# Three 256-column products of a weight tile onto one accumulator instead of a 512- and a 256-column product onto two halves

## The reference

```
hn = rmsnorm(x)
z, xbc, dt, u, g_a, g_b = split(hn @ w_in)
y_a = mamba2(z, silu(causal_conv(xbc)), dt) ; y_b = s5(u)
h  = x + (sigmoid(g_a) * y_a + sigmoid(g_b) * y_b) @ w_out
h  = h + (silu(gate) * val) @ w_down,   gate, val = causal_conv(rmsnorm(h) @ w_up)
out = rmsnorm(h)
```

## Time and profile before

| | us |
|---|---|
| three runs | 1672.95, 1673.08, 1673.11 |
| profiled execution | 1673.03 |
| its span, first to last instruction | 1671.3 |
| PE busy | 1661.6 |
| DVE busy | 1315.7 |
| ACT busy | 984.2 |
| mean granted clock of TensorE | 0.999 of full |

### The profile page before, as it was taken

One profiled execution on the slowest core, in us unless ns is written; L12 is line 12 of the kernel. 1 busy time (PEld: TensorE's weight loads), 2 busy tenths in 40 slices (PEclk: granted clock), 3 DMA queues, 4 the chain that ended last, 5 costly groups with the idle time before them and its releaser, 6 DMA issues.

```text
span 1671.3 us, 24189 instructions
## 1 busy us (share of the span) xinstructions
PE 1661.6 (99%) x8216; PEld 1386.3 (83%) x8216; DVE 1315.7 (79%) x1723; ACT 984.2 (59%) x1365; POOL 234.9 (14%) x337
## 2 busy tenths in 40 slices
PE   9999999999999999999999999999999999999998
PEld 8888888888888888888888888888888888888886
DVE  7999999999999996545766868888878888845544
ACT  7676676666677877444547754444444454454554
POOL 7843342221111110000000200000000000000001
PEclk9999999999999999999999999999999999999999
DMA  7666766666857666666787577777777777766564
GB/s 255 214 196 197 207 202 202 191 196 180 248 201 252 218 223 205 197 192 208 243 254 223 176 233 241 237 245 243 243 244 242 243 233 243 232 190 198 191 189 127
DMA packets 182873, 361.61 MB, mean 216 GB/s; under 512 B 17520, under 2 KB 45456, under 8 KB 182672
## 3 DMA queue, kind: packets, MB, share of 16 engines
q1 hardware_dynamic: 169264, 340.23, 64.0%
q0 software_dynamic: 12336, 19.92, 5.1%
q10 hardware_dynamic: 1200, 0.53, 0.1%
HBM read 335.41 MB, written 18.92 MB: 212 GB/s over the span
## 4 chain that ended last, share of the span: by engine, by line
PE 74%; DVE 2%; ACT 1%; issue 0%; DVEq 0%
PE psum L1930 23%; PE psum L1931 23%; PE psum L1932 23%; PE psum L1915 2%; PE psum L1917 1%; PE psum L2051 1%; DVE wlo L1216 1%; PE psum L2052 0%; DVE dec L1566 0%; ACT whi L740 0%; PE psum L2058 0%; PE psum L1966 0%; DVE dec L1562 0%; ACT xtok L949 0%; DVE zx L1629 0%
## 5 line engine op out<-in xcount | busy, mean ns | idle before, releaser
L740 ACT ACTIVATE whi<-raw 128x1024 fp32r<-128x1024 f32 x580 | 612.6, 1058 | 583.2 <-PE psum L1932 472.0
L1216 DVE TENSOR_TENSOR wlo<-raw,whi 128x1024 fp32r<-128x1024 f32 x580 | 708.8, 1228 | 312.6 <-ACT whi L740 305.9
L1915 PE MATMUL psum<-act,whi 128*128 128x512 f32 x1088 | 342.5, 396 | 0.0
L1930 PE MATMUL psum<-whi,nw 128*128 128x512 f32 x704 | 274.1, 389 | 0.0
L1931 PE MATMUL psum<-wlo,nw 128*128 128x512 f32 x704 | 273.9, 389 | 0.0
L1932 PE MATMUL psum<-whi,nw 128*128 128x512 f32 x704 | 273.9, 389 | 0.0
L1917 PEld LDWEIGHTS psum<-act,wlo 128*128 128x128 f32 x1088 | 204.4, 188 | 48.3
L1917 PE MATMUL psum<-act,wlo 128*128 128x256 f32 x1088 | 213.7, 278 | 0.0
L1915 PEld LDWEIGHTS psum<-act,whi 128*128 128x128 f32 x1088 | 165.6, 189 | 3.3 <-issue 3.2
L1932 PEld LDWEIGHTS psum<-whi,nw 128*128 128x128 f32 x704 | 132.1, 188 | 27.6
L1930 PEld LDWEIGHTS psum<-whi,nw 128*128 128x128 f32 x704 | 132.1, 188 | 27.3
(11 more groups left out here) (255 smaller groups left out, 2236.7 us busy)
## 6 DMA issues: line engine op xcount, KB each, us to landing
raw<-in_w_up SPq DMA_DIRECT2D x176, 512.0 KB, 4.8
raw<-in_w_zx SPq DMA_DIRECT2D x96, 512.0 KB, 3.7
raw<-in_w_down SPq DMA_DIRECT2D x88, 512.0 KB, 4.3
raw<-in_w_gate SPq DMA_DIRECT2D x64, 512.0 KB, 5.2
raw<-in_w_proj SPq DMA_DIRECT2D x48, 512.0 KB, 4.4
raw<-in_w_bc SPq DMA_DIRECT2D x32, 512.0 KB, 3.9
raw<-in_w_glu SPq DMA_DIRECT2D x32, 512.0 KB, 4.5
raw<-in_w_out SPq DMA_DIRECT2D x32, 512.0 KB, 4.7
```

Of the source, the lines that this page charges most:

```text
L740: fn(whi[:, s, :], raw[:, s, :], ACTF.Copy).then_inc(hi_ready, 1)
L1216: V.tensor_tensor(wlo[:, s, :], raw[:, s, :], whi[:, s, :], ALU.subtract).then_inc(lo_ready, 1)
L1915: mm(psum[:, b + t, :], whi[:, s, cols(t)], x, start=first, stop=False)
L1930: mm(banks[:, t, :], x_hi, high[:, k], start=first and k == 0, stop=False)
```

## The change

In `unit`, the 512-column matmul of the `whi` tile becomes two matmuls of 256 columns, first x_hi, then x_lo, and all products of a tile go onto the same 256 columns of PSUM. So a step is six matmuls of 256 columns. ScalarE copies the finished sums from PSUM straight to their place (for z, it applies SiLU in that pass), and increments `sum_ready` itself. The 36 VectorE adds and the semaphores `hsum_ready` and `z_done` go. At the end of `out`, VectorE adds the sums to `h` in one operation and waits for TensorE's `unit_used` alone.

```diff
-            def take_hsum(g, end, gi=0, ui=0):
+            def take_sums(to, g, end, gi=0, ui=0, func=ACTF.Copy):
 
                 act.wait_ge(unit_used, ui + end)
-                if g:
-                    act.wait_ge(sum_ready, gi + g)
-                fn(hsum[:, :, :], sums(g, 1), ACTF.Copy).then_inc(hsum_ready, 1)
+                fn(to, sums(g), func).then_inc(sum_ready, 1)
...
+            def group_sums(name, i, r):
+
                 _, per, quads, u0, g0 = phase(name)
-                take_hsum(g0 + r, u0 + (r + 1) * quads, i * per, i * (per * quads))
+                func = ACTF.Copy
+                if name == "u":
+                    to = ub[:, 2 * (r + 1):2 * (r + 1) + 2, :]
+                elif name == "zx" and r % 2 == 0:
+                    to, func = zx[:, ds(i * 4 + r, 2), 0, :], ACTF.Silu
+                elif comes_late(name, i, r):
+                    to = bc[:, i * 4 + r, :, :]
+                else:
+                    to = cpad[:, :, 3:3 + L]
+                take_sums(to, g0 + r, u0 + (r + 1) * quads, i * per, i * (per * quads), func)
...
-                if name == "zx" and r % 2 == 0:
-                    act.wait_ge(sum_ready, i * per + (g0 + r + 1))
-                    to = zx[:, ds(i * 4 + r, 2), 0, :]
-                    fn(to, to, ACTF.Silu).then_inc(z_done, 1)
...
-            def add_halves(to, g, gi=0):
-
-                dve.wait_ge(hsum_ready, gi + (g + 1))
-                V.tensor_tensor(to, sums(g, 0), hsum[:, :, :], ALU.add).then_inc(sum_ready, 1)
...
-                dve.wait_ge(hsum_ready, g + 1)
-                mul(hg, hg, hsum[:, :, :], ALU.add)
-                V.tensor_tensor(hg, sums(g, 0), hg, ALU.add).then_inc(sum_ready, 1)
+                dve.wait_ge(unit_used, UNIT0[name] + 4 * r + 4)
+                V.tensor_tensor(hg, sums(g), hg, ALU.add).then_inc(sum_ready, 1)
...
+                    x_hi, x_lo = x[:, 0:L], x[:, L:2 * L]
                     for t in tiles:
-                        mm(psum[:, b + t, :], whi[:, s, cols(t)], x, start=first, stop=False)
+                        mm(psum[:, b + t, 0:L], whi[:, s, cols(t)], x_hi, start=first, stop=False)
+                        mm(psum[:, b + t, 0:L], whi[:, s, cols(t)], x_lo, start=False, stop=False)
                     for t in tiles:
-                        ins = mm(psum[:, b + t, L:2 * L], wlo[:, s, cols(t)], x[:, 0:L], start=False, stop=last)
+                        ins = mm(psum[:, b + t, 0:L], wlo[:, s, cols(t)], x_hi, start=False, stop=last)
```

More of the change, by code:

```diff
@@ L242, in build_program @@
         dec_in = [sem("dec_in0"), sem("dec_in1")]
-        hi_ready, lo_ready, unit_used, hsum_ready, sum_ready = map(
-            sem, ("hi_ready", "lo_ready", "unit_used", "hsum_ready", "sum_ready"))
+        hi_ready, lo_ready, unit_used, sum_ready = map(
+            sem, ("hi_ready", "lo_ready", "unit_used", "sum_ready"))
         dve_step, act_step, pool_step, const_ready = map(sem, ("dve_step", "act_step", "pool_step", "const_ready"))
@@ L268, in build_program @@
         tap_ready = sem("tap_ready")
-        z_done, conv_done, xbc_done, cb_ready, scan_ready, exp_ready, m_ready, y_ready = map(
-            sem, ("z_done", "conv_done", "xbc_done", "cb_ready", "scan_ready", "exp_ready",
+        conv_done, xbc_done, cb_ready, scan_ready, exp_ready, m_ready, y_ready = map(
+            sem, ("conv_done", "xbc_done", "cb_ready", "scan_ready", "exp_ready",
                   "m_ready", "y_ready"))
@@ L303, in group_bank, with sums @@
             return 2 * (g % 2)
-        def sums(g, half):
+        def sums(g):
             b = group_bank(g)
-            return psum[:, b:b + 2, half * L:half * L + L]
+            return psum[:, b:b + 2, 0:L]
         def chunk_banks(name, c):
@@ L781, in _ @@
                 split_hi(n)
-            take_hsum(0, 4)
-            def group_hsum(name, i, r):
+            take_sums(ub[:, 0:2, :], 0, 4)
+            def group_sums(name, i, r):
                 _, per, quads, u0, g0 = phase(name)
-                take_hsum(g0 + r, u0 + (r + 1) * quads, i * per, i * (per * quads))
+                func = ACTF.Copy
[8 more added lines that the diff above has]
+                take_sums(to, g0 + r, u0 + (r + 1) * quads, i * per, i * (per * quads), func)
             def normed_hi(c):
@@ L814, in _ @@
                     if r >= 2 and j == 0:
-                        group_hsum("u", 0, r - 2)
+                        group_sums("u", 0, r - 2)
                     if j == 1:
@@ L858, in group_silu @@
                 _, per, quads, u0, g0 = phase(name)
-                if name == "u":
+                if name == "u" or name == "zx" and r % 2 == 0:
                     return
-                if name == "zx" and r % 2 == 0:
-                    act.wait_ge(sum_ready, i * per + (g0 + r + 1))
-                    to = zx[:, ds(i * 4 + r, 2), 0, :]
-                    fn(to, to, ACTF.Silu).then_inc(z_done, 1)
-                elif name == "zx":
+                if name == "zx":
                     act.wait_ge(conv_done, i * 2 + (r // 2 + 1))
@@ L896, in mixer_turn @@
                     last = name == "bc" and i == 1 and r == per - 1
-                    group_hsum(*before)
+                    group_sums(*before)
                     hi(0)
@@ L955, in gate_turn @@
                 if prev is None:
-                    group_hsum("bc", 1, 3)
+                    group_sums("bc", 1, 3)
                     hi(0)
@@ L988, in gate_turn @@
                     act.wait_ge(xbc_done, 18)
-                    act.wait_ge(z_done, 12)
+                    act.wait_ge(sum_ready, GROUP0["bc"])
                 hi(5)
@@ L1104, in _ @@
                 out_tail(s)
-                if s in (27, 31):
-                    take_hsum(GROUP0["out"] + s // 4 - 6, UNIT0["out"] + s + 1)
             def take_blocks(c, cc):
@@ L1295, in u_group @@
                 return GROUP0["u"] + r - 1 if r else GROUP0["u0"]
-            def u_sums(r):
-                add_halves(ub[:, 2 * r:2 * r + 2, :], u_group(r))
             def u_scaled(r):
@@ L1306, in lo @@
                 split_lo(UNIT0["u"] + j)
-            u_sums(0)
             dve.wait_ge(dt_half, 2)
@@ L1328, in _ @@
             V.reciprocal(s5p[:, 15, :], s5p[:, 14, :]).then_inc(s5_inv, 1)
-            u_sums(1)
             lo(9)
@@ L1336, in _ @@
             lo(12)
-            u_sums(2)
             normed(3)
@@ L1422, in s5_out @@
                 V.scalar_tensor_tensor(to, to, col("s5_d", blk), sums_at, ALU.mult, ALU.add).then_inc(y5_out, 1)
[L1424 to L1433, removed]
             def group_conv(name, i, r):
@@ L1467, in late_add @@
                     ins.then_inc(conv_done, 1)
[L1469 to L1474, removed]
             def x_turned(g):
@@ L1500, in mixer_turn @@
                     lo(0)
-                    if r or start:
-                        group_sums(*before)
                     s5_turn_back(r, blk * 4 + (r + 1), blk, start and r == 0)
@@ L1516, in mixer_turn @@
                         lo(2)
-                    cpad_free(*before)
                     s5_turn_on(r)
@@ L1520, in mixer_turn @@
                         last_state_sum(blk)
-                    if r == per - 1 and not last:
-                        group_sums(name, i, r)
                     if not last:
@@ L1586, in gate_turn @@
                     lo(0)
-                    group_sums("bc", 1, 3)
                     s5_out(7, YS5_LAST)
@@ L1623, in gate_turn @@
                     dve.wait_ge(xbc_done, 18)
-                    dve.wait_ge(z_done, 12)
+                    dve.wait_ge(sum_ready, GROUP0["bc"])
                 dve.wait_ge(y_ready, i * 2 + 2)
```

## The result

The changed kernel takes 1686.13 us (median of 6 runs, 1685.75 to 1686.40), the kernel before took 1673.09 us beside it (6 runs, 1672.80 to 1673.17). The ratio is 1.0078, with a 95% interval of 1.0065 to 1.0091: slower by 13 us, where the prediction had 1669.5 and a range up to 1677. The profiled execution has a span of 1684.0 us, and a mean granted clock of 0.998 of full against 0.999. Another execution of the changed kernel had 0.999 and took 1686.07 us, so the clock took no part.

The account below looks back on a forecast made before the run. The prediction took TensorE's matmul stream to bound the kernel, with no other engine holding it up. Profiled 1673.03 us, - 3.1 for the stream, - 0.4 for a removed wait, gave 1669.5 us; range 1663.5 to 1677.

Parts of the forecast that it names:

- A step after the change: Prediction's step pricing all six 256-column matmuls like L1917's, 0.1152 us each: 0.6914 us a step instead of 0.6965.
- the term of -3.1 us: TensorE's matmul stream: 0.0051 us saved in each of 608 steps.
- the far end: Slow case of 0.120 us for each matmul of a step, 1687 us in all; chance 3%.
- the fast rival: New 256s stream at half of `glu`'s 512, 0.1134 us; step 0.680, gain 9.8 us, 1662.8 us; chance 12%.
- its upper end: Upper bound on the matmul price from L1917's longest pair, 0.24 us: step 0.720 us, +14 us.
- the formula of the Trainium skill: Matmul distance N/2.4 ns plus fixed 2.5 ns: step from 650 to 655 ns, 608 steps cost 3.0 us more.
- What bounds the kernel: Claim that TensorE bounds the kernel, with 74% of the chain, and no other engine holds it up.
- Each matmul has a price of its own: Slower rival in the steps: two 256s 0.0036 us dearer than one 512, +4.4 us, 1677.0 us; chance 13%.
- The instruction stream: Slower rival: larger loop bodies of `zx` and `bc` cost 7 us at five jumps back, 1676.5 us; chance 5%.
- The wait of L2010: TensorE's 0.4 us wait for the sum into `cpad`, to go because ScalarE's copy frees the banks earlier.
- The relief: Less helper work, some 25 us on VectorE and 8.5 us on ScalarE, forecast to have no effect on time.
- The helpers' term of 0.4 us: Gain of 0.4 us forecast from removing TensorE's wait at L2010 for the sum into `cpad`.

Follow-up runs that it names:

- e1: Kernel before with only the 512-column matmul cut into two of 256, accumulator halves and VectorE adds kept: 1686.13 us, ratio 1.008.
- e3: Kernel before plus, before the end of `out`, unused streams of 24 matmuls per width (512 to 128 columns) and mixed steps in two orders: 1723.18 us.
- e5: Changed kernel with a step's six matmuls reordered so no tile is loaded twice in a row and accumulators alternate: 1685.99 us, ratio 1.008 against the kernel before.
- e7: Kernel before with each 512-column matmul of `glu` and `proj` cut into two of 256, 960 more matmuls: 1686.22 us, ratio 1.008.
- e2: Changed kernel with the old 512-column matmuls; ScalarE copies, no VectorE adds, W_hi·x_lo left out of the sums: 1672.39 us, ratio 0.9996 against the kernel before.
- e10: Changed kernel with 64 instead of 128 loaded columns in 532 of 608 steps: 1665.07 us, ratio 0.995 against the kernel before.
- e8: Kernel before plus unused streams of 24 matmuls by width and load size, then eight times two 512s and eight 256s: 1730.18 us.
- e9: Kernel before with 64 instead of 128 loaded columns in 532 of 608 steps: 1674.22 us, ratio 1.0005.
- e4: Kernel before with a step's four matmuls ordered 512, 256, 512, 256 instead of 512, 512, 256, 256: 1678.2 us, ratio 1.003.

## Why the prediction was wrong

**The step that failed** is the one under "A step after the change": "so 0.1152 is already the price with nothing saved up, and I take it for all six". A stream of nothing but such matmuls runs at 120 ns (the changed kernel, e1, e3, e5, e7), so the term of -3.1 us was +13.5; this is the far end that the prediction had worked out as 1687 and gave 3%. The 0.1152 was a correct reading of two distances and a wrong price: the step of 696.5 ns was divided at the borders of the rows, which made the 512s 233.0 and the 256s 115.2. Streams of one kind give 226.9 and 119.9, and 3.1 for the mixture: 453.8 + 239.8 + 3.1 = 696.7. The change trades this for 6 x 120 = 720: four 256s for two 512s, +26, and the mixture's 3 back.

**The rows allowed the other division.** `glu` had the 512 in a pure stream, 0.2268. Taking it out of the step twice leaves (696.5 - 453.6) / 2 = 121.5 for a 256, and six of those make +20 us. The prediction used that row to argue for the fast rival, that the 512s could be freed of a slowness, and took the price from single distances where it should have kept both divisions of the sum. It had 0.24 / 2 as its upper end, which is what came, and set it aside. For the same reason it dismissed the formula of the Trainium skill against the split: it held two 256s of the mixed step, 0.2305 us, against one 512 of it, 0.2330. The pure streams say 239.8 ns against 226.9, so the formula had the sign right, and with 3.0 us a loss four times too small.

**What bounds the kernel** was read rightly, on thinner ground than the prediction says. The chain with 74% TensorE begins at 378 us and says nothing of `u`, `zx` and half of `bc`, where 1007 of the 1216 matmuls of L1915 stand; there the reading rests on the waits alone. The runs bear it out: e1 has the whole loss with the helpers as they were, and e2, with the new helpers and the old matmuls, has none.

**The rivals.** "Each matmul has a price of its own" was right in its kind, wrong in its size and in its supposed reason: no reload of x_lo's tile is involved (e5), and nothing of the activation's side (e7). The fast rival is refuted for whole tiles: what the 512s gain by leaving the mixture is 3.1 ns a step. That half tiles give its 113 and its 0.680 (e10) goes with the smaller load. The instruction stream did not run dry: 3.8 us of "issue" in 10 waits against 4.6 in 9, and no gap at the jump.

**What held.** Loads and matmuls, 9432 each. The wait of L2010, gone, though not for the reason given: it is gone in e1 too, where the helpers are as before. No effect of the helpers (e2). Untouched token-major stages: 226.7 ns from start to start in `glu`, before and after. The relief: busy time fell by 18.5 us on VectorE and 5.9 on ScalarE, where 25 and 8.5 were forecast, but busy time counts overlapping instructions once; their durations add up to 23.7 and 8.3 us less. It was worth as little as forecast.

**The sum.** From start to next start, the matmuls of all 608 steps take 426.1 us before and 439.7 after, or +13.5: 22.3 ns a step over the whole kernel, a little less than the 23.5 at the end of `out`. The small S5 matmuls of L1999 take 9.1 us before and 8.6 after, which is 0.5 back. Together that is the 13.0 measured. The helpers' term of 0.4 us is in no run clear of noise: e2 has 0.65 without the split, but e1, with the old helpers, has the same 439.7, the same 8.6, and the same 1686.13 as the changed kernel.

**What stays open.** Why 512 and 384 columns pay 13 to 18 ns also behind small loads, why a mixture is dearer in some orders and cheaper in another (e8), and why wide matmuls are slow for a while behind narrow ones, no run here tells. For 256 columns it is shown that 6.7 of the 13.3 ns go with the size of the load (or of the result, which shrinks with it); the other half is not explained.

## What to carry to other kernels

The distance between two starts in a mixed stream is not the price of the matmul in front: only the sum over a period is. Take a pure stream of each kind as its price, and if only one kind has one, divide the sum both ways and keep both ends as bounds. The pure prices gave the sums of the mixed periods here to within 2% with whole tiles. In this kernel's form (128 loaded columns, fp32r) one matmul of 512 columns beats two of 256 by 13 ns, while relief of ScalarE and VectorE is worth nothing as long as TensorE waits for neither.

## What the runs showed of the hardware that was not expected

- Behind a load of 128 columns, 224 columns and fewer all cost 111.5 to 111.7 ns (e3); behind one of 64, 128 columns took 60.0.
- A smaller load lowers the price at 256 columns (120, 116, 114, 113) but raises it at 512 (227, 230, 230, 232) (e8), and a mixed step with half tiles is slower than with whole ones, 700 against 697 ns (e9).
- The order of the same four matmuls is worth 5 us in 1673 (e4), and a period of two 512s and eight 256s is cheaper than its pure prices, 1406.6 against 1413.0 ns (e8).
- TensorE's loads show 188 ns in wide streams and 192 where they trail the 256s, and are hidden or not without a wait of any kind in the profile: this loss has no row of its own.
